# A decoder step on one core: the gates of tiles 2 to 7 as seven half-depth block products per pair of tiles, with the arrays around them moved

## What is computed

```python
def in_projection(h, norm_g, w_in, b_gate):
    xn = rmsnorm(h, norm_g)
    parts = jnp.split(xn @ w_in, SPLIT_POINTS, axis=-1)
    gates = tuple(jax.nn.sigmoid(parts[9 + i] + b_gate[i]) for i in range(N_BRANCH))
    return parts[0:3], parts[3:6], parts[6:9], gates
...
def merge_and_mlp(h, gates, y_a, y_b, y_c, w_out, norm_mlp_g, w_up, w_down):
    mixed = gates[0] * y_a + gates[1] * y_b + gates[2] * y_c
    h = h + mixed @ w_out
    hn = rmsnorm(h, norm_mlp_g)
    return h + jnp.square(jax.nn.relu(hn @ w_up)) @ w_down
```

## Time and profile before

| | |
|---|---|
| median of 3 runs | 1008.75 us (1008.74 to 1009.38) |
| the profiled execution | 1010.09 us, of it the span 1006.8 us |
| TensorE's mean granted clock in it | 0.998 of full speed |
| PE, DVE, ACT, POOL busy | 98%, 58%, 44%, 31% of the span |
| matmuls x mean | 8426 on PE, most of 0.28 us, pipelined |

### The profile page before, as it was taken

One profiled execution on the slowest core, in us unless ns is written; L12 is line 12 of the kernel. 1 busy time (PEld: TensorE's weight loads), 2 busy tenths in 40 slices (PEclk: granted clock), 3 DMA queues, 4 the chain that ended last, 5 costly groups with the idle time before them and its releaser, 6 DMA issues.

```text
span 1006.8 us, 21775 instructions
## 1 busy us (share of the span) xinstructions
PE 986.1 (98%) x8426; PEld 914.7 (91%) x8426; DVE 587.9 (58%) x1042; ACT 439.8 (44%) x858; POOL 312.6 (31%) x180
## 2 busy tenths in 40 slices
PE   7999999999999999999999999999999999999996
PEld 7988787797787787899999999999999999999995
DVE  6214478799355556253444475777847947873334
ACT  6114656677244332252233324465346436424532
POOL 2333233222312221012211112244634445354720
PEclk9999999999999999999999999999999999999999
DMA  8589977756797676624222326537576586469102
GB/s 301 181 274 320 336 260 237 289 204 207 264 334 238 224 241 202 241 84 169 89 101 85 105 89 226 204 138 266 218 262 257 215 282 250 159 261 359 61 1 85
DMA packets 65671, 209.47 MB, mean 208 GB/s; under 512 B 7833, under 2 KB 10138, under 8 KB 63266
## 3 DMA queue, kind: packets, MB, share of 16 engines
q1 hardware_dynamic: 65282, 207.75, 58.7%
q10 hardware_dynamic: 288, 0.35, 0.2%
HBM read 200.59 MB, written 51.48 MB: 250 GB/s over the span
## 4 chain that ended last, share of the span: by engine, by line
PE 93%; DVE 4%; issue 1%; ACT 1%; DMA 0%; DVEq 0%; ACTq 0%
PE G L1658 61%; PE S L1658 14%; PE Z L1658 13%; PE TR L1661 2%; PE OU L1658 2%; DVE pw L1496 1%; DVE mtmp L1201 1%; DMA xraw<-in_xt_dram 0%; DVE macc L1198 0%; DVE psp L1201 0%; PE TR L1658 0%; DVE share L1547 0%; DVE dvT L1198 0%; ACT mixh L878 0%; DVE pT L1505 0%
## 5 line engine op out<-in xcount | busy, mean ns | idle before, releaser
L1658 PE MATMUL G<-xh,whi 128*128 128x260 f32 x1288 | 372.3, 289 | 7.9 <-DVE xl L1201 7.2
L1658 PE MATMUL G<-xl,whi 128*128 128x260 f32 x1288 | 364.7, 283 | 0.0
L1658 PE MATMUL G<-xh,wlo 128*128 128x260 f32 x1288 | 364.4, 283 | 0.0
L844 POOL TENSOR_TENSOR wlo<-wraw,whi 128x1024 fp32r<-128x1024 f32 x60 | 148.4, 2474 | 477.2 <-ACT whi L878 477.2
L1658 PEld LDWEIGHTS G<-xh,whi 128*128 128x128 f32 x1288 | 243.5, 189 | 38.3 <-issue 32.3
L1658 PEld LDWEIGHTS G<-xl,whi 128*128 128x128 f32 x1288 | 243.7, 189 | 0.0
L1658 PEld LDWEIGHTS G<-xh,wlo 128*128 128x128 f32 x1288 | 243.6, 189 | 0.0
L878 ACT ACTIVATE whi<-wraw 128x1024 fp32r<-128x1024 f32 (+1 forms) x84 | 88.0, 1048 | 204.4 <-PE G L1658 186.0
L840 POOL TENSOR_TENSOR wlo<-mraw,whi 128x512 fp32r<-128x512 f32 x60 | 81.0, 1374 | 95.2 <-ACT whi L878 95.2
L854 POOL TENSOR_TENSOR mlow<-mraw,bhigh 128x512 fp32r<-128x512 f32 x36 | 57.9, 1626 | 66.0 <-DVE bsum L1198 58.9
L1198 DVE TENSOR_TENSOR tg<-G,rstd 128x260 f32<-128x260 f32 x48 | 20.5, 427 | 78.7 <-PE G L1658 78.7
(11 more groups left out here) (329 smaller groups left out, 2227.9 us busy)
## 6 DMA issues: line engine op xcount, KB each, us to landing
wraw<-in_w_in_dram SPq DMA_DIRECT2D x65, 512.0 KB, 5.7
kv<-in_kpool_dram SPq DMA_DIRECT2D x128, 256.0 KB, 3.7
kv<-in_vpool_dram SPq DMA_DIRECT2D x128, 256.0 KB, 3.5
mraw<-in_w_up_dram SPq DMA_DIRECT2D x32, 512.0 KB, 5.7
out_win_k_kept_dram<-in_cache_win_k_dram SPq DMA_DIRECT2D x8, 2047.0 KB, 11.3
out_win_v_kept_dram<-in_cache_win_v_dram SPq DMA_DIRECT2D x8, 2047.0 KB, 11.5
mraw<-in_w_down_dram SPq DMA_DIRECT2D x30, 512.0 KB, 3.5
wraw<-in_w_ab_dram SPq DMA_DIRECT2D x8, 512.0 KB, 3.2
```

The costliest lines, as they stand in the source:

```text
L844: nc.gpsimd.tensor_tensor(low(u), raw(u)[0], high(u).bitcast(F32), ALU.subtract).then_inc(w_lo, 1)
L1658: return nc.tensor.matmul(out, lhsT, rhs, start=start, stop=stop, **kw)
```

## The change

- `make_units`: the gates of tiles 0 and 1 stay; those of tiles 2 and 3, 4 and 5, 6 and 7 become the kind `sgate`, nine *pairs* q = 0 to 8 (pair of tiles, and gate within it). Gates of 2 and 3 (q = 0 to 2) come before the first `yc`, those of 4 and 5 (q = 3 to 5) after `w_ab` of tile 1, those of 6 and 7 (q = 6 to 8) after `w_ab` of tile 3.
- Each pair is seven ticks `gprod` of half depth (12 matmuls) in the order `GSEQ` = (0, 4, 2, 3, 1, 5, 6); the last two, 5 and 6, are put behind the first product of the pair that follows, or behind the first two ticks of `yc` or of ya. Plain gate ticks of these tiles are 9 x 4 of 24 matmuls before.
- The accumulators: products 0, 2, 1, 5 share one, 3 and 6 a second, 4 has the third. Products 2, 1, 5 go on summing into what the product before left there, so PE waits for `g_copied`, ACT's copy of that accumulator (after products 0, 2 and 1) into `tg`, and product 6 for DVE's taking of product 1. DVE adds a copy to an accumulator (4, 1, 6), scales the sum by `rstd` in a second instruction, and ACT makes the tanh; product 5 is scaled alone.
- Weights: the four sums of a pair are made by DVE from `wraw` (`gsum`, a ring of six), in the order of `G_SUMS`; ACT makes seven high halves of 512 columns (`ghigh`, a ring of six), DVE the low halves of products 2 and 1 (`gslow`), POOL those of 0, 4, 3, 5, 6 (`glow`, `gslow`). The table `_ticks` hangs these steps on the ticks of the pair before (for q = 0, 3, 6 on the ticks ahead of its first product; `_f` is that tick).
- The input's differences: four arrays `xd1` to `xd4` of 1040 columns, in the space of the page buffers of the paged cache; two of them by POOL (`x_odd`, three instructions each), two by DVE (`x_even`, two each); ACT splits all four (`x_hi`), DVE makes the low halves (`x_lo`).
- The page stages of the attention over the cache (`v_ticks`) stand 2.5 ticks apart instead of 3, `branch_split` stands earlier, `x_again` only after the last gate product, and arrays of the MLP lie elsewhere.

```diff
-    for t in range(4):
+    def gate_pairs(t):
+        for b in range(3):
+            for n in range(2):
+                unit("sgate", 2 * (3 * (t // 2 - 1) + b) + n, "w_in", GA + 8 * b + t + n, KC, [])
+    for t in range(2):
         gates(t)
+    gate_pairs(2)
     for half in range(2):
         unit("c", half, "w_c", half, KC, [("yc", 2 * i, 2, "dil", 4 * half + i) for i in range(4)])
         for t in range(4 * half, 4 * half + 4):
             unit("ab", t, "w_ab", t, KC, [("ya", 0, 4, "conv", t), ("yb", 4, 4, "sb", t)])
-            if half == 0:
-                gates(t + 4)
+            if t in (1, 3):
+                gate_pairs(t + 3)
...
+    if _unit["kind"] == "sgate":
+        if _unit["tile"] % 2 == 0:
+            _q = _unit["tile"] // 2
+            _seven = [(_u, ("gprod", 0, KC // 2, None, _q), _j, _j == 6) for _j in GSEQ]
+            TICKS += _seven[:1] + _late + _seven[1:5]
+            _late = _seven[5:]
+        continue
...
+            if _late and (_job[0] == "ya" or _h):
+                TICKS += _late
+                _late = []
...
+G_SUMS = (0, 1, 3, 2)
+G_DVE = (2, 1)
+G_POOL = (0, 4, 3, 5, 6)
+G_HIGHS, G_SUM_RING = 6, 6
...
+    if _q % 3:
+        _k = [gate_tick(_q - 1, n) for n in range(7)]
+        _ticks = (_k[1:7] + [_next], [_k[1], _k[1], _k[3], _k[4]], [_k[4], _k[6]], [_k[1], _k[2], _k[4], _k[6], _next])
...
+    else:
+        _ticks = ([_f - 6, _f - 6, _f - 5, _f - 4, _f - 4, _f - 3, _next], [_f - 6, _f - 6, _f - 5, _f - 4], [_f - 4, _f - 2],
+                  [_f - 6, _f - 5, _f - 4, _f - 2, _next])
...
+    elif _k >= GATED_TICK:
+        _j = TICKS[_k][2] if _job[0] == "gprod" else None
+        if _j in (2, 1, 5, 6):
+            BANK.append(BANK[at("gprod", _job[4], 3 if _j == 6 else 0)])
+        else:
+            BANK.append(_free.pop(0))
+        if _j in (None, 4, 5, 6):
+            _free.append(BANK[-1])
...
-        v_ticks.append(v_ticks[-1] + 3)
+        v_ticks.append(v_ticks[-1] + 2.5)
...
+    t = at("cb", 3) + 2
     for n in range(len(BRANCH_TILES)):
-        add(l_end - 1 + 0.5 * n if n < 8 else max(l_end + 3, v_end + 7) + 0.5 * n - 4, "branch_split", n)
-    add(BRANCH_TICK + 4, "x_again")
+        add(t + 0.5 * n if n < 4 else v_end + 4 + 0.5 * (n - 4) if n < 8 else max(v_end + 6, l0 + LSTEPS + 8) + 0.5 * (n - 8),
+            "branch_split", n)
+    for n in range(2):
+        add(t + 2.5 * n, "x_odd", n)
+        add(t + 3 + n, "x_even", n)
...
+    add(gate_tick(GPAIRS - 1, 6) + 1, "x_again")
...
+                elif u >= WR and gated(u - WR):
+                    q, odd = UNITS[u - WR]["tile"] // 2, UNITS[u - WR]["tile"] % 2
+                    sp.wait_ge(g_summed, 4 * q + 4)
+                    sp.wait_ge(g_lo_pool, 5 * q + (5 if odd else 2))
...
+                sp.wait_ge(made, gate_tick(GPAIRS - 1, 6) + 1)
...
+            def gate_low_pool(q, n):
+                j = G_POOL[n]
+                if q == 0 and n == 0:
+                    pool.wait_ge(xd_lo, 3)
+                    await_taken(pool, "s_red", 0)
+                pool.wait_ge(g_hi, 7 * q + GSEQ.index(j) + 1)
+                if j in PLAIN_AT and q:
+                    pool.wait_ge(made, at("gprod", q - 1, j) + 1)
+                nc.gpsimd.tensor_tensor(gate_low(q, j), gate_raw(q, j), gate_high(q, j).bitcast(F32),
+                                        ALU.subtract).then_inc(g_lo_pool, 1)
...
+            def gate_seven(k, q, j):
+                b, t = gate_tiles(q)
+                if j in (0, 2, 1):
+                    if j == 0 and b == 0:
+                        await_gate_parts(act, t)
+                    act.wait_ge(made, k + 1)
+                    copy(gate_part(t + (j > 0), b, j % 2), bank[BANK[k]][:, 0:HALF]).then_inc(g_copied, 1)
+                if j not in (0, 2, 3):
+                    if j == 5:
+                        act.wait_ge(*took(k))
+                    else:
+                        act.wait_ge(g_scaled, 3 * q + (4, 1, 6).index(j) + 1)
+                    tile, h = t + (j in (1, 6)), int(j in (1, 5))
+                    part = gate_part(tile, b, h)
+                    nc.scalar.activation(part, part, ACT.Tanh, scale=0.5, bias=bgate[:, b, tile:tile + 1]).then_inc(tanh_made, 1)
...
+            def gate_hi(q, n):
+                j = GSEQ[n]
+                if q == 0 and n == 0:
+                    act.wait_ge(l_done, 2)
+                    act.wait_ge(s_v_made, 1)
+                    act.wait_ge(xd_lo, 3)
+                if j in SUM_AT:
+                    act.wait_ge(g_summed, 4 * q + G_SUMS.index(SUM_AT.index(j)) + 1)
+                else:
+                    act.wait_ge(*raw(gate_plain(q, PLAIN_AT.index(j))[0])[1:])
+                m = 7 * q + n - G_HIGHS
+                if m >= 0:
+                    act.wait_ge(made, gate_tick(m // 7, m % 7) + 1)
+                copy(gate_high(q, j), gate_raw(q, j)).then_inc(g_hi, 1)
...
+                tt(out, xh[:, part[0], part[1]].bitcast(F32), less, ALU.subtract).then_inc(xd_even, 1)
+                dve.wait_ge(xd_even, 2 * n + 1)
+                tt(out, out, xl[:, part[0], part[1]].bitcast(F32), ALU.add).then_inc(xd_even, 1)
...
+                m = 4 * q + i - G_SUM_RING
+                if m >= 0:
+                    dve.wait_ge(made, at("gprod", m // 4, SUM_AT[m % 4]) + 1)
+                if n:
+                    dve.wait_ge(g_summed, 4 * q + n)
+                first, second = gate_raw(q, SUM_AT[0]), gate_raw(q, SUM_AT[1])
+                a, b, op = ((odd[0][:, top], odd[0][:, end], ALU.add), (first, even[0][:, top], ALU.subtract),
+                            (even[0][:, top], odd[0][:, top], ALU.subtract), (even[0][:, end], second, ALU.subtract))[i]
+                tt(gate_raw(q, SUM_AT[i]), a, b, op).then_inc(g_summed, 1)
...
+            def take_gate(k, q, j):
+                if j not in (4, 1, 5, 6):
+                    return
+                b, t = gate_tiles(q)
+                h = int(j in (1, 5))
+                dst, root = gate_part(t + (j in (1, 6)), b, h), rstd[:, half(h)]
+                src = bank[BANK[k]][:, 0:HALF]
+                if b == 0 and j == 4:
+                    await_gate_parts(dve, t)
+                if j != 5:
+                    dve.wait_ge(g_copied, 3 * q + (4, 6, 1).index(j) + 1)
+                dve.wait_ge(made, k + 1)
+                if j == 5:
+                    tt(dst, src, root, ALU.mult).then_inc(dve_took, 1)
+                    return
+                if j == 1:
+                    src = bank[BANK[at("gprod", q, 3)]][:, 0:HALF]
+                tt(dst, src, dst, ALU.add).then_inc(dve_took, 1)
+                dve.wait_ge(*took(k))
+                tt(dst, dst, root, ALU.mult).then_inc(g_scaled, 1)
...
+            def gate_product(k, part, q, j):
+                if part == 0:
+                    if j in G_DVE:
+                        pe.wait_ge(g_lo_dve, 2 * q + G_DVE.index(j) + 1)
+                    else:
+                        pe.wait_ge(g_lo_pool, 5 * q + G_POOL.index(j) + 1)
+                    if q == 0 and j in (1, 2, 3, 6):
+                        pe.wait_ge(xd_lo, (2, 3, 6, 1).index(j) + 1)
+                    if j in (2, 1, 5):
+                        pe.wait_ge(g_copied, 3 * q + (2, 1, 5).index(j) + 1)
+                    elif j == 6:
+                        pe.wait_ge(*took(at("gprod", q, 1)))
+                    else:
+                        pe.wait_ge(*took(PREV[k]))
```

282 lines of the change are left out of this document (220 added, 62 removed).

## The result

The changed kernel took 1030.07 us, median of four runs (1026.6 to 1031.29), against 1008.95 (1008.74 to 1009.38) for the kernel before on the same chip: a ratio of 1.0203, 95% interval 1.0176 to 1.023. The forecast was slower, 1023, with a range to 1031: the direction is right, and the 21 us that the change costs are 7 more than the 14.4 of the sum, close to the upper end. The profiled execution took 1031.29, its span 1029.4, 22.6 us above the 1006.8 of before.

The account below looks back on a forecast made before the run. PE's matmuls were taken to bound the kernel, the other engines hidden. 12.3 us saved against 26.7 lost in gaps gave +14.4 on the median of 1008.75, so 1023 us, range 1001 to 1031 (the walk's own 1012 to 1031).

Parts of the forecast that it names:

- the sum: Over the whole kernel: 26.7 us lost in gaps on PE, 12.3 saved by the nine pairs, so +14.4.
- first entry: Second tick of g0 of tile 0 to product 2 of pair 0: DVE falls behind, 7.7 us lost.
- second: The eight ya and yb ticks ahead of pair 3: DVE falls behind, 4.5 us lost.
- third: Before pair 6, with POOL's tile half a tick earlier and DVE 0.5 ahead: 4.0 us lost.
- windows: Pairs 0, 1, 3, 4, 6, 7, under which the next pair is prepared: 7.7 us lost for six.
- the clash: yc(0,1) and yc(4,1) get the accumulator of the tick just before: 1.9 and 0.85, together 2.75 us lost.
- DVE busy over 90% between the gates of tile 0 and pair 2: Sign of being right: DVE nearly full there, from 42.6 us of work and turns in 42.5.
- the other signs: Among them: DVE's `gslow` and `gsum` well over 0.68, and POOL's low half ending gaps at product 0 of pairs 1, 2, 4, 5, 7, 8.
- the lower bound: Time if DVE's waits for turns were half of those taken: 14 us lost, 1010.
- Covered after all: PE waits only when DVE lags over 2.9 us: 7 lost, 1003.5 us, or 996.5 with no loss; chance 0.22.
- Weights late: Raw weights arrive too late for DVE; each of six windows loses 1 to 2 more: 1032 us; chance 0.04.
- Half lost: DVE's waits for turns are half of those taken: 14 us lost, 1007 to 1011 us; chance 0.06.

Follow-up runs that it names:

- pool_half: The changed kernel with POOL's five low halves of each pair made over half of their columns only: 1017.36 us.
- spread_quarter: Changed kernel with late_one's edit, six pairs in one row, preparation spread out, page stages 3 ticks apart, POOL's low halves over a quarter of columns: 1008.16 us.
- pool_quarter_late: late_one with POOL's five low halves of each pair made over a quarter of their columns only: 1011.13 us.
- late_one: The changed kernel with products 5 and 6 of pairs 2 and 8 behind the first yc tick instead of the second: 1023.05 us.

## Why the prediction was right, and where it wasn't

**The direction and the gaps.** The direction and the mechanism were those forecast: operations of DVE with two SBUF inputs and POOL's take turns. The sum of the gaps was forecast at 26.7 and came out at 26.1. Term by term: first entry 8.15 for 7.7, second 4.08 for 4.5, third 3.95 for 4.0, windows 6.23 for 7.7. That the sum agrees to 0.6 us is partly luck: windows 1.5 too high and the clash 1.7 too low cancel. pool_half and spread_quarter, with the durations, show that the windows are lost to POOL's turns (4.8 of 6.2); for the entries pool_half and pool_quarter_late show it for 3.5 to 4.2 of 8.0. That the rest is DVE's and ACT's own row of work is argued; no run shortened it.

**A sign that failed.** I had given "DVE busy over 90% between the gates of tile 0 and pair 2" as a sign of being right, from 42.6 us of work and turns in 42.5. It was busy 76%. The first entry's 7.7 came out at 8.15, but not because DVE is full: DVE and ACT wait for each other (5.7 us for ACT's branch splits alone), and 5.1 of the 5.4 at pair 0 stay in pool_half. The size was right there, its reason only in part. Of the other signs, `gsum` was well over 0.68 (0.93 to 1.29), `gslow` was not (0.681), and pair 1 had no wait for POOL's low half. The matmuls in the traces are 8426 and 8318, 108 less as forecast; 7818 and 7710 stand in no trace.

**The clash at `yc`** was mis-sized: 2.75 forecast, 4.49 measured, of it 2.26 at yc(4,1) for 0.85 and 2.23 at yc(0,1) for 1.9. The scaling in front is a two-input operation, and I had given it its lone duration at the one place where POOL makes a whole low half of 2.4 beside it.

**The clock** is the term that the sum left out. I had worked with 0.119 from matmul to matmul throughout, since the trace of before had 1.00 in every stretch. A gap has its own price and may have that of the lower clock behind it: after the 4.2 us at pair 0 and the 2.35 us at the first `yc` some 1.4 us each, and at the first gates 3.1. With the slower first matmuls behind each gap it makes 9.5 us in the profiled execution. That is why the span grew by 22.6 and not by 14.4: the gaps are 0.6 under it, the matmuls saved 0.6 more (12.9 for the 12.3 of the sum), and 9.5 stand against it. The runs of one kernel lie 4.7 us apart, and their clock goes with the time (0.996 at 1026.6, 0.990 at 1031.3).

**The windows by pair** were not as I had placed them. I had 1.1 and 1.45 in the two windows of a group; measured were none and 1.37 in the first group, 0.77 and 1.37 in the other two, and 0.19 in the last pair of each.

**Its working.** Two steps are a little off: 2 x 1.29 + 1.1 - 0.8 is 2.9 and not 2.8, which makes the second wait of a window 0.9 to 1.4, and the lower bound was worked out as 1010 and then used as 1012. Neither moves the forecast.

**The rivals.** "Covered after all" fell: its point of decision, DVE more than two results behind, was reached at each entry. "Weights late" played no part; no wait of PE or DVE here ended with a load of `wraw`. "Half lost" fell as well: even pool_half has 18.9 us of gaps for its 14.

**What stays open.** What makes the clock fall at the first gates, without a gap in front. It was seen with the page stages at 2.5 ticks (in six of the eleven profiled executions), and in none of the three at 3, but no run varied that distance with all else kept in a kernel that shows it often. How far another order for ACT would shorten the entries was tried only once, and a version that beats the kernel before was not found.

## What to carry to other kernels

Price an algebraic saving on TensorE by what the other engines do in its window: here a pair saves 1.37 us and its window costs up to 1.37 (1.04 on average), because operations of DVE with two SBUF inputs and POOL's exclude each other. A sum of busy times over a period doesn't tell it; list which operations stand side by side, and give every DVE operation with two SBUF inputs that starts beside a POOL operation the rest of that operation as well. Look too at which engines wait for each other in turn: an engine can be late at 76% busy. And where a forecast opens gaps on a TensorE that had none, add the slower clock behind each long one, and a wider range upwards.

## What the runs showed of the hardware

- The granted clock fell to its lower level behind gaps of 4.2 and 2.35 us (ended at 448.9 and 480.2), but not behind the one of 2.38 at 588.0 of the same execution, nor behind single ones of 1.0 to 1.9. Behind the first the matmuls were 0.217 apart from 450.1 to 453.4 and 0.119 after. In late_one, without the gap at the first `yc`, it doesn't fall there.
- It also fell without such a gap, in the first gates, twice in the changed kernel's profiled execution (0.58 from 388 to 392 us, 0.64 from 396 to 400) for 3.1 us of loss, and not in late_one's. What makes it fall there is open.
- Which of DVE's two-input operations pays for POOL is set by what stands beside it: sums 0.93 to 1.29 for 0.68, scalings 0.64 for 0.43, low halves none here, and 1.27 for 0.68 in the `down` pairs. A held sum of 512 columns ended 0.55 after POOL's operation, a held one of 260 columns 0.29 after.
